# A two-block transformer layer on one core: V centred by a product where it is turned, the scan's output left in its bank, the identity added behind the keys' mask, the gated scan's low-rank input made feature-major

## The reference, cut to what matters

```python
def wkv7_scan(state, inputs, reverse):
    def step(S, xs):
        r, w, k, v, a, b = xs
        sa = jnp.einsum('bhvk,bhk->bhv', S, a)
        S = S * w[:, :, None, :] + sa[..., None] * b[:, :, None, :] + v[..., None] * k[:, :, None, :]
        return S, jnp.einsum('bhvk,bhk->bhv', S, r)
...
def rwkv_readout(y, inputs, r_k, gn_g, gn_b):
...
    mu = jnp.mean(y, -1, keepdims=True)
    var = jnp.mean(jnp.square(y - mu), -1, keepdims=True)
    yn = ((y - mu) * lax.rsqrt(var + GN_EPS)).reshape(B, T, RWKV_W) * gn_g + gn_b
    bonus = jnp.sum(r * k * r_k, -1, keepdims=True) * v
    return yn + bonus.reshape(B, T, RWKV_W)
```

```python
h = rms_norm_2(x, norm_g[l, 0])
q, k, v, g, lr, u_f, u_h, u_s = jnp.split(h @ w_in[l], split_at, axis=-1)   # lr: 2 * 16 columns
gk_fwd = log_sigmoid(lr[..., :16] @ gk_w[0] + gk_b[0]) / 16.0
gk_bwd = log_sigmoid(lr[..., 16:] @ gk_w[1] + gk_b[1]) / 16.0
```

## Time and profile before

| | |
|---|---|
| median of the runs | 3786.3 us (3 runs, 3783.22 to 3786.93) |
| span of the profiled execution | 3776.6 us; it has no time of its own beside this |
| TensorE busy, share of the span | 3522.4 us, 93% |
| VectorE busy | 2039.3 us, 54% |
| ScalarE busy | 1541.7 us, 41% |
| GpSimd busy | 247.0 us, 7% |
| mean granted clock of TensorE | 0.971 of full speed |
| bytes read from HBM | 535.86 MB, 144 GB/s |

### The profile page before, as it was taken

One profiled execution on the slowest core, in us unless ns is written; L12 is line 12 of the kernel. 1 busy time (PEld: TensorE's weight loads), 2 busy tenths in 40 slices (PEclk: granted clock), 3 DMA queues, 4 the chain that ended last, 5 costly groups with the idle time before them and its releaser, 6 DMA issues. The chain is left out here.

```text
span 3776.6 us, 70993 instructions
## 1 busy us (share of the span) xinstructions
PE 3522.4 (93%) x31292; PEld 2922.0 (77%) x31292; DVE 2039.3 (54%) x3564; ACT 1541.7 (41%) x2599; POOL 247.0 (7%) x295
## 2 busy tenths in 40 slices
PE   6798999999999989899999899989999999999998
PEld 3576777777767767777887788658998899999887
DVE  1354465456444666764656465655444555555444
ACT  2343343344333433455543443435333444444433
POOL 0001111111011130011100000010000000000000
PEclk9999999999999999999999799899999999999999
DMA  9433343334323245433335444334553555555554
GB/s 378 157 115 102 105 121 108 95 118 124 102 85 103 71 152 192 156 123 101 101 114 178 156 150 134 106 106 158 188 169 132 167 180 181 182 182 180 190 185 161
DMA packets 349473, 548.57 MB, mean 145 GB/s; under 512 B 11724, under 2 KB 119916, under 8 KB 346988
## 3 DMA queue, kind: packets, MB, share of 16 engines
q1 hardware_dynamic: 346716, 538.78, 43.8%
q10 hardware_dynamic: 2448, 5.24, 0.4%
HBM read 535.86 MB, written 8.13 MB: 144 GB/s over the span
## 5 line engine op out<-in xcount | busy, mean ns | idle before, releaser
L301 PE MATMUL lane<-r,r 128*128 128x256 f32 (+1 forms) x8520 | 1506.4, 326 | 53.0 <-DVE r L259 43.0
L301 PE MATMUL bank<-r,r 128*128 128x512 f32 (+2 forms) x6360 | 1399.6, 359 | 61.5 <-DVE r L259 25.3
L301 PEld LDWEIGHTS lane<-r,r 128*128 128x128 f32 x8520 | 1279.2, 193 | 209.8 <-DVE r L259 48.0
L259 DVE TENSOR_TENSOR r<-ring,r 128x1024 fp32r<-128x1024 f32 x770 | 939.7, 1227 | 808.9 <-ACT r L298 807.5
L301 PEld LDWEIGHTS bank<-r,r 128*128 128x128 f32 x6360 | 1052.2, 195 | 262.7 <-ACT arena L298 30.6
L298 ACT ACTIVATE r<-ring 128x1024 fp32r<-128x1024 f32 x770 | 808.7, 1055 | 769.1 <-PE lane L301 572.3
L301 PE MATMUL lane<-arena 64*64 64x64 f32 (+4 forms) x12940 | 618.5, 252 | 44.6 <-issue 12.7
L301 PEld LDWEIGHTS lane<-arena 64*64 64x64 f32 (+3 forms) x12940 | 465.0, 138 | 208.4 <-issue 121.9
L298 ACT ACTIVATE arena<-lane 128x256 f32<-128x256 f32 (+3 forms) x578 | 249.1, 451 | 577.5 <-PE lane L301 453.5
L270 DVE COPY arena<-lane 128x256 f32<-128x256 f32 (+3 forms) x366 | 131.9, 361 | 281.4 <-PE lane L301 256.1
L259 DVE TENSOR_TENSOR arena<-arena 128x256 f32<-128x256 f32 (+7 forms) x568 | 260.1, 489 | 35.7 <-ACT arena L298 14.1
(11 more groups left out here) (94 smaller groups left out, 1233.6 us busy)
## 6 DMA issues: line engine op xcount, KB each, us to landing
ring<-in_w_gate_up SPq DMA_DIRECT2D x88, 1024.0 KB, 5.0
ring<-in_mod_w SPq DMA_DIRECT2D x73, 1024.0 KB, 5.2
ring<-in_ev_w_in SPq DMA_DIRECT2D x44, 1024.0 KB, 8.3
ring<-in_w_down SPq DMA_DIRECT2D x44, 1024.0 KB, 5.0
ring<-in_od_w_in SPq DMA_DIRECT2D x40, 1024.0 KB, 5.0
ring<-in_w_in SPq DMA_DIRECT2D x40, 1024.0 KB, 5.1
ring<-in_w_xkv SPq DMA_DIRECT2D x32, 1024.0 KB, 5.3
ring<-in_ev_w_out SPq DMA_DIRECT2D x28, 1024.0 KB, 5.2
```

What stands on the lines that cost most here:

```text
L259: return Nothing() if self.e is None else self.e.tensor_tensor(o, a, b, op)
L301: return Nothing() if self.e is None else self.e.matmul(o, l, r, start=start, stop=stop)
```

## The change

**Step turn_AV.** The two tiles of v are no longer transposed but multiplied: v is the stationary operand, `cen_bd` the moving one, so that the bank gets v turned and centred. TensorE does this before it waits for A. The scan then runs on centred values, and y comes out centred.

**Steps state3 to read_out.** ScalarE squares y straight out of its bank; the copy `s.y` is gone. The bank is kept until VectorE has multiplied by it in read_out. The step centre is now bonus: only the product with `ones_bd`, into the second bank of the lane's pair. VectorE makes the bonus without waiting for ScalarE's square.

**Steps P_LR and KR.** The three identity adds move from behind LR's mask to behind the keys' mask.

**The low-rank input.** One group by `feats` with 32 columns: the weights' 32 columns are stationary and the 256 tokens move. `lr_turned` is gone. One tile holds 32 features, both directions; `gkw[d]` is 32 rows high, with zeros in the other direction's 16 rows, which GpSimd writes first, and SyncE waits for that.

```diff
@@ order_of_work: unit
-        b = bank(t)
-        step("centre", d, n, by, b)
+        step("bonus", d, n, bank(pair_turns[d][1]))
         yield "centre"
         b2 = bank(pair_turns[d][0])
-        step("gn_sum", d, n, b, b2)
+        step("gn_sum", d, n, by, b2)
         yield "gn_sum"
-        step("read_out", d, n, b, b2)
+        step("read_out", d, n, by, b2)
...
-    to_gla = stream([rows("hF0", KT, [0, 1], "w_in_2", W2_LR, 32, "lr_in", (), lambda: step("lr_turned", bank(aux))),
+    to_gla = stream([Group("hF0", KT, [0], "w_in_2", W2_LR, 32, "lr_in", (), None, True, None),
@@ SyncE: load_mix
         for d in range(2):
-            load(f"gkw{d}", M.gkw[d][0:16, :], I["gla_gk_w_2"][0, d])
+            sp.wait_ge(*sp.table.at("gkw_zero", d))
+            load(f"gkw{d}", M.gkw[d][16 * d:16 * d + 16, :], I["gla_gk_w_2"][0, d])
@@ TensorE
     def turn_AV(d, n, b):
         s = M.lane[d]
-        turn4(b, [s.AR[:, 0, 0, :], s.AR[:, 1, 0, :], s.v[:, 0:P], s.v[:, P:2 * P]], ("v", d, n), ("A", d, n))
+        fresh(b)
+        pe.wait_ge(*at("v", d, n))
+        for c in range(2):
+            pe.mm(M.bank[b[0]][:, T + c * P:T + c * P + P], s.v[:, c * P:c * P + P], C("cen_bd"), True, True)
+        pe.wait_ge(*at("A", d, n))
+        for c in range(2):
+            i = pe.tr(M.bank[b[0]][:, c * P:c * P + P], s.AR[:, c, 0, :], ident)
+        i.then_inc(*pe.n(("full", *b)))
...
-    def centre(d, n, by, b):
+    def bonus(d, n, b):
         s = M.lane[d]
         fresh(b)
-        pe.wait_ge(*at("y", d, n))
-        pe.mm(M.bank[b[0]][:, 0:256], C("cen_bd"), s.y, True, True)
         pe.wait_ge(*at("rk", d, n))
-        pe.mm(M.bank[b[0]][:, 256:512], C("ones_bd"), s.t1, True, True).then_inc(*pe.n(("full", *b)))
+        pe.mm(M.bank[b[0]][:, 0:256], C("ones_bd"), s.t1, True, True).then_inc(*pe.n(("full", *b)))
...
-    def lr_turned(b):
-        fresh(b)
-        pe.wait_ge(*at("lrr", 1))
-        for d in range(2):
-            for tl in range(2):
-                i = pe.tr(M.bank[b[0]][0:16, (2 * d + tl) * P:(2 * d + tl + 1) * P], M.lrr[:, tl, 16 * d:16 * d + 16], ident)
-        i.then_inc(*pe.n(("full", *b)))
@@ TensorE: gl_gate
-        pe.mm(M.bank[b[0]][:, 0:T], M.gkw[d][0:16, hp * P:hp * P + P], M.lr[d][0:16, :], True, True) \
+        pe.mm(M.bank[b[0]][:, 0:T], M.gkw[d][0:32, hp * P:hp * P + P], M.lr[0:32, :], True, True) \
@@ VectorE
             .then_inc(*v.n(("free", *bp[0]), ("free", *bp[1]), ("LR", d, n, 0)))
-        own()
+
+    def plus_one(s, d, n):
+        v.wait_ge(*at("LR", d, n, 0))
         v.tt(s.Z[1][:, 0, :, 1, :], s.LR[:, :, 0, 0, :], M.C("i64").unsqueeze(1).to_broadcast([P, 2, 64]), ADD) \
             .then_inc(*v.n(("TT1", d, n)))
...
@@ VectorE: KR
                  M.SI[d].unsqueeze(1).to_broadcast([P, 4, P]), MUL).then_inc(*v.n(("free", *b), ("KR", d, n)))
+            plus_one(s, d, n)
...
-        v.wait_ge(*at("gn_sq", d, n))
-        v.tt(s.t1, M.bank[b[0]][:, 256:512], s.v, MUL).then_inc(*v.n(("bonus", d, n)))
...
+        v.tt(s.t1, M.bank[b[0]][:, 0:256], s.v, MUL).then_inc(*v.n(("free", *b), ("bonus", d, n)))
@@ VectorE: read_out
-        v.tt(s.yc, s.yc, M.bank[b[0]][:, 0:256], MUL).then_inc(*v.n(("free", *b)))
+        v.wait_ge(*at("gn_sq", d, n))
+        v.tt(s.yc, s.yc, M.bank[by[0]][:, 256:512], MUL).then_inc(*v.n(("free", *by)))
@@ ScalarE: state3
-            a.act(s.y, M.bank[by[0]][:, 256:512], ACT.Copy).then_inc(*a.n(("free", *by), ("y", d, n)))
+            a.act(s.ysq, M.bank[by[0]][:, 256:512], ACT.Square).then_inc(*a.n(("gn_sq", d, n)))
...
-    def lr_in(b, tl):
-        copied(b, M.lrr[:, tl, :], ("lrr", tl))
-
-    def lr_turned(b):
+    def lr_in(b, f):
         full(b)
-        for d in range(2):
-            a.act(M.lr[d][0:16, :], M.bank[b[0]][0:16, d * T:d * T + T], ACT.Copy).then_inc(*a.n(("free", *b), ("lr",)))
+        a.act(M.lr[0:32, :], M.bank[b[0]][0:32, 0:T], ACT.Copy).then_inc(*a.n(("free", *b), ("lr",)))
@@ GpSimd: load_mix
+        for d in range(2):
+            g.zero(M.gkw[d][0:32, :]).then_inc(*g.n(("gkw_zero", d)))
```

More of the change, by code:

```diff
@@ L620, in layout @@
     M.oacc = gp.take(2 * 512).rearrange("p (t n) -> p t n", t=2)
-    M.lr = [sp.take(T) for _ in range(2)]
+    M.lr = sp.take(T)
     M.gkw = [sp.take(T) for _ in range(2)]
-    M.lrr = sp.take(64).rearrange("p (t n) -> p t n", t=2)
     M.glg = sp.take(P)
@@ L1853, in state, with gn_sum, read_out @@
         m.then_inc(*pe.n(("y_mm", d, n, i)))
[L1855 removed]
+    def bonus(d, n, b):
         s = M.lane[d]
         fresh(b)
[L1858 to L1859 removed]
         pe.wait_ge(*at("rk", d, n))
[L1861 to L1863 removed]
+        pe.mm(M.bank[b[0]][:, 0:256], C("ones_bd"), s.t1, True, True).then_inc(*pe.n(("full", *b)))
+    def gn_sum(d, n, by, b2):
         pe.wait_ge(*at("gn_sq", d, n))
         head_sums(b2, M.lane[d].ysq, C("head_mean"), "gn_sum", d, n)
[L1867 removed]
+    def read_out(d, n, by, b2):
         pe.wait_ge(*at("gn_rs", d, n))
@@ L1893, in times_w @@
                 if g.feats:
-                    c = slice(f * P, f * P + P)
+                    c = slice(f * P, min(f * P + P, g.n))
                     r_hi, r_lo = M.pairs[pair].cols(kk)
                     l_hi, l_lo = hi[:, j, c], lo[:, j, c]
-                    o = M.bank[b[0]][:, 0:T]
+                    o = M.bank[b[0]][0:c.stop - c.start, 0:T]
                 else:
@@ L2162, in tensor_program @@
         start, mod, mod_col, ev_times, lora, kk_sum, keys, turn_AV, P_LR, KR, double, KV,
-        turn_BK, solve, QY, GH, state, centre, gn_sum, read_out,
+        turn_BK, solve, QY, GH, state, bonus, gn_sum, read_out,
         combine, first_done, times_w, pool_mix, pool_done, gate_row, lat_done, ctx_done, h1, h1_done, v_rows, k_turned, q_turned,
-        scores, p_turned, values, attended, rms, rms_turned, lr_turned, gla_ready, gl_gate, gl_scores, gl_states, gl_out,
+        scores, p_turned, values, attended, rms, rms_turned, gla_ready, gl_gate, gl_scores, gl_states, gl_out,
         to_mix, fn_channels, fn_tokens, sc_sum, sc_out, x3_done, hy_one, hy_two, hy_taps, hy_filter, hy_rows, hy_there,
@@ L2382, in solve, with bonus, read_out @@
         v.stt(s.t1, s.r, M.vcol("r_k", hp), s.kp, MUL, MUL).then_inc(*v.n(("rk", d, n)))
-    def centre(d, n, by, b):
+    def bonus(d, n, b):
         s = M.lane[d]
         full(b)
-        v.wait_ge(*at("gn_sq", d, n))
-        v.tt(s.t1, M.bank[b[0]][:, 256:512], s.v, MUL).then_inc(*v.n(("bonus", d, n)))
-    def read_out(d, n, b, b2):
+        v.tt(s.t1, M.bank[b[0]][:, 0:256], s.v, MUL).then_inc(*v.n(("free", *b), ("bonus", d, n)))
+    def read_out(d, n, by, b2):
         s, (hp, seg) = M.lane[d], divmod(n, 2)
@@ L3061, in vector_program @@
     take = {f.__name__: f for f in (
-        start, mod_col, h0, ev_split, lora_shift, gate_in, shift, kk_sum, keys, P_LR, KR, double, solve, QY, GH, state, centre,
+        start, mod_col, h0, ev_split, lora_shift, gate_in, shift, kk_sum, keys, P_LR, KR, double, solve, QY, GH, state, bonus,
         read_out, combine, first_done, split_w, split, pool, pool_mix, pool_done, gate_diag, add_first, ctx_done,
@@ L3668, in scalar_program @@
     take = {f.__name__: f for f in (
-        start, mod_row, h0, ev_split, lora_in, lora_shift, rkv_in, gate_in, shift, kk_sum, gn_sum, state, turn_AV, double, KV, turn_BK, solve, centre, read_out,
+        start, mod_row, h0, ev_split, lora_in, lora_shift, rkv_in, gate_in, shift, kk_sum, gn_sum, state, turn_AV, double, KV, turn_BK, solve, read_out,
         combine, spill_out, first_done, split_w, pool, pool_done, gate_row, norm0_q, h1, h1_done, to_q, to_k, to_v,
         k_rows, v_rows, q_rows, hn_square, hn_scale, k_turned, q_turned, scores, p_turned, gate_heads, attended, norm1, rms,
-        rms_turned, lr_in, lr_turned, qk_in, vg_in, gla_ready, gl_gate, gl_spread, gl_scores, gl_norm, to_mix, us_in, uf_in,
+        rms_turned, lr_in, qk_in, vg_in, gla_ready, gl_gate, gl_spread, gl_scores, gl_norm, to_mix, us_in, uf_in,
         fn_channels, fn_tokens, uh_in, load_fg, add_x, hy_one, hy_two, hy_taps, hy_sides, hy_filter, hy_rows, hy_there, hy_norm,
@@ L3729, in solve, with gn_sum, read_out @@
              s.dc[:, 0:4].unsqueeze(2).to_broadcast([P, 4, 64]), MUL).then_inc(*g.n(("DI", d, n)))
-    def gn_sum(d, n, b, b2):
+    def gn_sum(d, n, by, b2):
         g.wait_ge(*at("gn_in", d, n))
         power(M.lane[d].dc[:, 8:12], "gn_pow", d, n)
-    def read_out(d, n, b, b2):
+    def read_out(d, n, by, b2):
         g.here("unit_end", d, n, "pool")
```

## The result

The changed kernel takes 3760.8 us (median of 4 runs, 3760.3 to 3764.9), the kernel before 3784.8 (4 runs, 3779.5 to 3786.9). The ratio is 0.9940, with a 95% interval of 0.9926 to 0.9954, which is 22.7 us (17 to 28) less; by the two medians it is 24.0. The forecast was 23.2 us less, 3763.1 us. Two later timings of the same kernel beside before gave 0.9944 (0.9931 to 0.9956) and 0.9937 (0.9925 to 0.9950).

What follows compares the result with a forecast made beforehand. TensorE was taken to set the pace of the scan. The terms -7.0 - 1.0 + 0 - 15.2 = -23.2 gave span 3753.4 and time 3763.1 us, 0.6% faster, range 3751 to 3775.

Steps and rivals of the forecast that it cites:

- the 9.7 us around the span: Whole kernel: median of the runs 3786.3 less the profiled span 3776.6, added unchanged to the new span.
- Part 3: Low-rank input: 48 records moving 256 columns at full clock replace 96 records and four transposes; -15.2 us.
- The two rivals on the clock: Low-rank product: the clock falls again in it (0.15, 3767.3 us), or does not rise at 2096.7 (0.05, 3765.1 us).
- Part 1: turn_AV and centre, 32 units: 0.45 us saved, 0.23 added on TensorE in each; -7.0 us.
- The case that products of v cost as much as those of 256 columns: turn_AV: moving the centring saves nothing, the term becomes +8 us, time 3778; chance 0.04.
- The end of the last unit: End of the scan, fill used up: copy and product leave the chain; -1.0 us, between 0 and -2.
- Part 2: Identity adds moved behind the keys' mask, on VectorE: 0 booked; a loss at most 0.93 us a unit, 30 us.
- in front of the first copy there are three adds instead of six: VectorE before the doubling's first copy: fewer adds stand ahead with the move; part of the reasoning for booking 0.
- the bound of 0.93 us a unit: Identity adds on VectorE: most that late adds could lose in each of 32 units, 30 us in all.
- The limit of 2.8 us: Scan: TensorE's wait for VectorE's masks and adds in 1220 us, so the adds' move can gain no more.
- The slower rival: Bonus product waits for its bank in the first segment's 16 units; with 2 us, +32, time 3795; chance 0.03.
- The zeros and SyncE's wait: Low-rank input: GpSimd's zeros delay small loads and weight pieces some 2 us; booked at 0, +2 without cover.

Runs made afterwards that it cites:

- e1: The kernel before with the feature-major low-rank input alone; 3764.4 us, ratio 0.9954 to before.
- e2: The kernel before with turn_AV, state3, bonus and read_out changed (centring alone); 3770.5 us, ratio 0.9969 to before.
- e5: The changed kernel with four more float32 products of 128x256 in each of the 32 bonus steps; 3806.6 us, ratio 1.0067 to before.
- e6: The changed kernel with the two products of v made five times in each unit; 3817.3 us, ratio 1.0096 to before.
- e3: The kernel before with the three identity adds moved behind the keys' mask alone; 3781.9 us, ratio 0.9999 to before.
- e8: The changed kernel with the identity adds back behind LR's mask; 3755.4 us, ratio 0.9935 to before.
- e11: The changed kernel with the identity adds back behind LR's mask, timed again beside the changed kernel; 3758.2 us, ratio 0.9926 to before.
- e9: The kernel before with its old low-rank product placed behind q and k instead of in front; 3780.2 us, ratio 0.9990 to before.

## Why the prediction was right, point by point

- **The whole.** -23.2 forecast, -22.7 measured (-17 to -28), time 3763.1 against 3760.8. The difference was to the median, as it should be; only the 9.7 us around the span were mistaken, 1.8 being right. Made strictly on the trace, the sum would have given 3755.2 for the profiled execution, which took 3760.8. That the whole came within 0.5 us is luck: the interval is 5 us each way, and by the traces the parts are 15.2 less in the low-rank input and some 6 less for the centring, with some 3 more for the identity adds that the forecast held at 0. That makes 18 to 19; the rest of the 22.7 was not found in one place, and the interval covers it.
- **Part 3, -15.2.** The trace has -15.2, e1 -17.4 (-12 to -22). Clock, price of a record and readiness of hF0 were as said. The two rivals on the clock did not come about: it neither fell in the product nor rose late. Here again 18 transposes filled the stretch ahead of the rise (2094.70 to 2098.10, above), and the clock was at 1.00 in the next. The Trainium skill ("TensorE: Matmul & The Clock Gate", Part 4) has it that transposes do not count as busy for the clock. This trace disagrees, as that of before did.
- **Part 1, -7.0.** By the rows -5.4 to -6.4: 0.42 saved and 0.22 to 0.28 added, where 0.45 and 0.23 were forecast. By the table of scans -6.4, an estimate that holds the end of the last unit too, where the forecast for both was -8.0. By e2 -11.7 (-7 to -17), at whose edge it lies. e5 and e6 confirm both prices, and that TensorE's time is the scan's. The case that products of v cost as much as those of 256 columns is excluded by e6.
- **The end of the last unit, -1.0.** It came to about -0.6. In the changed kernel the wait of 1.04 us in front of centre is gone, and in front of the transposes that turn the widened result back stands one of 2.37 instead of 0.92. In the first fence after, in the second before:

```profile
1354.50 0.56 PE L301 MATMUL lane<-arena 64*64 64x64 f32 x12
...
1359.62 0.44 PE L304 MATMUL lane<-cm,arena 128*128 128x128 f32 x2 [2.37 <-ACT arena L298]
1359.89 0.51 PE L301 MATMUL lane<-cm,arena 128*128 128x2 f32 x4
```

```profile
1355.12 0.56 PE L301 MATMUL lane<-arena 64*64 64x64 f32 x12
...
1361.10 0.60 PE L301 MATMUL lane<-cm,arena 128*128 128x2 f32 x4
```

  From the first row to the last it is 5.4 us, against 6.0 before. What left TensorE came back as a longer wait for ScalarE, which the -1.0 had not counted.
- **Part 2, 0.** For the move alone the number holds by e3 (0.9999), the reasoning does not. The step "in front of the first copy there are three adds instead of six" looked at lane 0 only. In front of lane 1's first copy there are three adds where there had been none behind the mask, and the bound of 0.93 us a unit was for this. The limit of 2.8 us, too, was read from the waits of TensorE's products alone; the loads of the stationary tiles already waited 13.4 us for the same line before the change (`PEld lane L301 <- DVE arena L259: 13.4, 40, 0.8`, 220 to 1350 us). These waits grew by 4 to 7 us. In time the move costs 2.9 us in the changed kernel by the table of scans, and 0 to 4 by the medians.
- **The slower rival.** The bonus never waited: its group of 64 records has 0.0 us of idle time before it in the whole span:

```profile
L301 PE MATMUL lane<-arena,cm 128*128 128x256 f32 x64 | 20.5, 402 | 0.0
```

- **The zeros and SyncE's wait**, booked at 0. SyncE issues the loads of `gkw` 1.99 us after the load ahead of them, where it was 0.38; its queue in order of time, before and after:

```profile
2087.27 0.34 SPq L307 DMA_DIRECT2D arena<-in_k_mix  x1
2087.65 0.90 SPq L307 DMA_DIRECT2D arena<-in_gla_gk_w  x2
```

```profile
2088.73 0.34 SPq L307 DMA_DIRECT2D arena<-in_k_mix  x1
2090.72 0.81 SPq L307 DMA_DIRECT2D arena<-in_gla_gk_w  x2
```

  It costs nothing that shows: the rows of TensorE from 2098.53 to 2107.23 above have no wait, and TensorE's waits from 2090 to 2300 us add up to 24.5 us before and 24.4 after, 20.0 of each ahead of the transposes of hF0.

Of the kernels run, the one without the identity move, e8 and e11, is the quickest that computes all of it: 3755.4 and 3758.2 us against 3761.3 and 3762.0 of the changed kernel. The lead is within the uncertainty of either timing; it has the direction that the table of scans gives.

## What to carry to other kernels

Price a narrow product not by its records alone but by the granted clock in the rows of it and of what follows it. A correction that is linear, such as taking a mean away, can ride on a transpose that is made anyhow: here 0.22 us more for 0.42 less. And when work is moved behind another instruction, list for every lane what then stands between that instruction and the next one that someone waits for.

## What the runs showed that was not expected

- The clock was low for longer than the narrow records lasted. In e9 v's records of 512 columns began at 2144.50, and the clock was 0.50 until 2149.50, 20.5 us after it fell at 2129.00; before the change it was down from 2100.10 to 2120.60, also 20.5 us, with q and k of 256 columns in the last 4.6. So in both it came back 20.5 us after the fall and 4.6 to 5.0 us after the first wide record. The narrow product is equally long in both, so these two cases cannot tell which of the two distances counts. It is not how long every fall lasts: of the 36 stretches at 0.50 in the trace of before, 31 lasted under 7 us.
- A product with a 32-column stationary tile and 128 or 256 moved columns kept the clock at 1.00. The prediction had held the narrow tile for a reason against.
- The same kernel differs from run to run by more than its parts: e3's eleven runs go from 3775.1 to 3787.3 us, and the scan's end by 10 us between three traces. Most of the latter is how long the clock stood at 0.50; taken into account, parts of 3 us could be read from traces where the times could not tell them.
